# Gelu and gate product of the expert rows in groups of two instead of eight

## What is computed

```python
def peer_ffn(h, w_q, keys, u, v):
    ...                      # queries, keys, top-k: for each token 8 heads x 16 experts = 128 ids and gates g
    def block(args):
        xt, et, gt = args
        act = jax.nn.gelu(jnp.einsum('td,thkd->thk', xt, u[et]), approximate=False)
        return jnp.einsum('thk,thkd->td', gt * act, v[et])
```

## Time and profile before

| | us |
|---|---|
| median of 3 runs | 4148.64 |
| lowest, highest | 4130.71, 4150.37 |
| the profiled execution | 4132.56 |
| its span (first to last instruction) | 4130.5 |
| PE / DVE / ACT / POOL busy | 3102.1 / 2438.0 / 823.3 / 2296.8 |

### The profile page before, as it was taken

One profiled execution on the slowest core, in us unless ns is written; L12 is line 12 of the kernel. 1 busy time (PEld: TensorE's weight loads), 2 busy tenths in 40 slices (PEclk: granted clock), 3 DMA queues, 4 the chain that ended last, 5 costly groups with the idle time before them and its releaser, 6 DMA issues.

```text
span 4130.5 us, 44027 instructions
## 1 busy us (share of the span) xinstructions
PE 3102.1 (75%) x11080; PEld 1750.8 (42%) x11080; DVE 2438.0 (59%) x5947; ACT 823.3 (20%) x1936; POOL 2296.8 (56%) x2101
## 2 busy tenths in 40 slices
PE   6864788668875888677885688757897578876666
PEld 5453345253442535354452545425454344532222
DVE  5236654947467565756558474675647656476444
ACT  2100321114111221113211141112311123111111
POOL 1004675646655575556755466554566556566776
PEclk9976899889987999888998899878898799988888
DMA  6447899898998899898998889988899888989998
GB/s 219 129 128 252 311 383 374 303 339 319 386 344 312 322 385 377 310 343 320 373 362 311 323 317 376 339 317 300 301 386 341 311 298 308 398 316 334 360 365 322
DMA packets 425232, 1333.42 MB, mean 323 GB/s; under 512 B 47616, under 2 KB 48768, under 8 KB 424320
## 3 DMA queue, kind: packets, MB, share of 16 engines
q0 software_dynamic: 294912, 1073.87, 70.4%
q1 hardware_dynamic: 128896, 252.28, 17.1%
q10 hardware_dynamic: 1152, 4.19, 0.3%
HBM read 1320.46 MB, written 9.70 MB: 322 GB/s over the span
## 4 chain that ended last, share of the span: by engine, by line
PE 42%; DVE 21%; issue 19%; DMA 9%; ACT 4%; another core or an unknown queue 3%; POOL 2%; DVEq 0%; POOLq 0%; ACTq 0%; SPq 0%
PE ps_sum L990 20%; PE ps_p L771 9%; DMA rows<-in_peer_v,ids_v 4%; DVE rows L1692 4%; PE ps_s L912 4%; DMA w_ring<-in_wstream 3%; DVE feat_b L1595 3%; DVE feat_b L1590 2%; PE ps_s L855 2%; DVE e L1597 1%; PE ps_p L863 1%; POOL rows L591 1%; POOL rows L582 1%; PE ps_t L762 1%
## 5 line engine op out<-in xcount | busy, mean ns | idle before, releaser
L990 PE MATMUL ps_sum<-rows,diag 128*128 128x512 f32 x3584 | 1864.5, 657 | 561.6 <-ACT diag L1230 405.4
L582 POOL DMA_INDIRECT rows<-in_peer_u,ids_u x1024 | 1128.2, 1102 | 1231.4 <-issue 584.3
L591 POOL DMA_INDIRECT rows<-in_peer_v,ids_v x1024 | 1152.1, 1125 | 584.0 <-issue 311.0
L1692 DVE CUSTOM_DVE_ANT_0 rows<-rows,h_cur 128x1024 f32<-128x1024 f32 x1024 | 1224.0, 1221 | 182.6 <-DMA rows<-in_peer_u,ids_u 156.5
L990 PEld LDWEIGHTS ps_sum<-rows,diag 128*128 128x128 f32 x3584 | 710.6, 211 | 1445.6 <-issue 1033.8
L771 PEld LDWEIGHTS ps_p<-hT,w_ring 128*128 128x128 f32 x3968 | 513.7, 207 | 128.5 <-issue 90.0
L771 PE MATMUL ps_p<-hT,w_ring 128*128 128x128 f32 x3968 | 524.4, 292 | 47.1 <-DMA w_ring<-in_wstream 29.9
L1230 ACT ACTIVATE diag<-ident,acts 128x128 f32<-128x128 f32 x896 | 317.5, 392 | 818.0 <-PE ps_sum L990 327.2
L762 PE MATMUL ps_t<-ident,xs 128*128 128x128 f32 x192 | 45.1, 412 | 263.0 <-DVE xs L1404 183.3
L1707 DVE SCALAR_TENSOR_TENSOR x_cur<-rows,acts,x_cur 128x1024 f32<-128x1024 f32 x128 | 164.4, 1285 | 119.6 <-DMA rows<-in_peer_v,ids_v 111.1
L1500 DVE CUSTOM_DVE_ANT_0 e<-ps_s,bias_t 128x512 f32<-128x512 f32 (+3 forms) x96 | 82.2, 856 | 235.5 <-PE ps_s L851 108.7
(11 more groups left out here) (263 smaller groups left out, 2372.2 us busy)
## 6 DMA issues: line engine op xcount, KB each, us to landing
w_ring<-in_wstream SPq DMA_DIRECT2D x816, 256.0 KB
bias_t<-bias_rows SPq DMA_DIRECT2D x40, 512.0 KB
rows<-in_peer_u,ids_u POOLq DMA_INDIRECT x1024
rows<-in_peer_v,ids_v POOLq DMA_INDIRECT x1024
bias_rows<-rows SPq DMA_DIRECT2D x5, 1024.0 KB, 9.5
bias_t<-in_x SPq DMA_DIRECT2D x8, 512.0 KB
out<-x_cur ACTq DMA_DIRECT2D x8, 512.0 KB
e<-in_final_gain SPq DMA_DIRECT2D x7, 512.0 KB
```

Source lines behind the costliest of these rows:

```text
L582: pool.indirect_dma_start(u_rows[:, j % G_RING, :], None, peer_u, bass.IndirectOffsetOnAxis(ap=ids_u[:, j:j + 1], axis=0)).then_inc(u_land ...
L591: pool.indirect_dma_start(v_rows[:, j % G_RING, :], None, peer_v, bass.IndirectOffsetOnAxis(ap=ids_v[:, j:j + 1], axis=0)).then_inc(v_land ...
L990: ins = pe.matmul(ps_sum[:, c * 512:(c + 1) * 512], diag[:, n % 4, :], v_rows[:, j % G_RING, c * 512:(c + 1) * 512], start=(n == 0), stop= ...
L1692: dve.tensor_tensor_reduce(row, row, h_cur[:, :], 1.0, 0.0, ALU.mult, ALU.add, dots[:, p:p + 1]).then_inc(u_used, 1)
```

## The change

`STEP`, the size of a group of Gelu and gate product, goes from 8 to 2, and the three lags that were written as `STEP` plus a number are written as the numbers that they had. So 64 Gelus and 64 products are made in a block instead of 16 each, each of 2 columns instead of 8, and the positions of dot product, diagonal, sum and gather stay. `GATE_LAG` stays 1.

```diff
-STEP = 8
+STEP = 2
...
-DIAG_LAG = STEP + 2
-SUM_LAG = STEP + 3
-GATHER_LAG = STEP + 4
+DIAG_LAG = 10
+SUM_LAG = 11
+GATHER_LAG = 12
```

## The result

The changed kernel takes 4204.7 us in the median of four runs (4199.76 to 4215.87) beside 4149.51 us (4130.71 to 4155.33) for the kernel before, a ratio of 1.0157 with an interval of 1.0125 to 1.0189. It is slower, inside the range of 4120 to 4255 us, and by more than the forecast said: +55 us between the medians and +67.4 us between the profiled spans (4197.9 against 4130.5), where the sum gave +37. The ratio is the recorded one; the two medians alone would give 1.0133, which lies inside its interval.

What follows compares the result with a forecast made beforehand. No engine is full; a PE, DVE, ACT chain bounds attention, PE the mixing, DVE the choice. Gates 25, attention 7 and choice 5 gave 37 us on 4132.56: 4169.6 us, 4186 on the median's scale; range 4120 to 4255 us.

Steps and rivals of the forecast that it cites:

- the forecast case: Whole kernel: slower by +21 to +60 us, given a chance of 0.45.
- Gates: Gates and recurrence: a diagonal waits behind row 27's Gelu, L829 3.6 us later per block; 25 us, bounds 9 and 46.
- Attention: Six other table loads per block, 7.7 us of ACT, mostly hidden: 1 us a block, 7 us in all, bounds 0 and 54.
- The cover of the loads: Attention: loads are free where ACT waits anyway, 46.6 us in 9 of 12 Exps, so 1 us a block.
- The wait for the dot product: ACT: diagonals wait for dot products instead of gate products, four times as often; no gain booked, cost only in the gates.
- Choice: Choice of top-k: nine more products on a full DVE at 0.08 us, 5 us over seven passes, upper bound 10.
- the rival on locks: ACT stands behind copies waiting for PE, at projections and two query products, holding DVE: 74 us more; chance 0.13.
- Start of a block: DVE finishes rows 8 and 9 2.3 us later, but weights get the queues: 0 taken, bounds -21 and +35 us.
- Hidden anyway: Rival: the gates' 3.6 us is regained before the scores or at block start; 4145 or 4161 us, chance 0.30.
- Faster: Rival: products seven positions ahead free PE, a quarter of ACT's 233.7 us returns; -46 us, about 4102 us, chance 0.12.
- Every load and every lock counts: Rival: DVE is held by ACT behind copies waiting for PE, 74 us more; 4244 or 4260 us, chance 0.13.
- The other sign of being wrong: Outside the choice: the forecast is wrong if PE's idle time in front of diagonals does not grow.

Runs made afterwards that it cites:

- lock8: Kernel before plus, on ACT at each odd position, a wait for that row's dot product; no load, Gelu or product added: 4158.54 us, ratio 1.0066.
- loads8: Kernel before plus a Gelu of constant data, waiting for nothing, at each odd position without its own; 180 table loads: 4162.16 us, ratio 1.0077.
- c2: Changed kernel (groups of two) with a plain copy in place of the Gelu, 34 table loads, output not the reference's: 4167.68 us, ratio 1.0083.
- c8: Kernel before (groups of eight) with a plain copy in place of the Gelu, 34 table loads, output not the reference's: 4104.6 us, ratio 0.9935.
- mid8: Changed kernel with rows 24 to 63 back in groups of eight, groups of two elsewhere: 4156.65 us, ratio 1.0046.
- prod6: Changed kernel with each gate product four positions later, Gelus unmoved: 4238.79 us, ratio 1.0206.
- c_both2: Changed kernel with copies for Gelus, the copy three positions later and the product four behind it: 4153.95 us, ratio 1.0025.

## Why the prediction came out as it did

**Right in sign and range, short in size.** It said +37 us with +21 to +60 as the forecast case; the medians say +55, the ratio 4149.51 x 0.0157 = 65 us, and the profiled executions 67. So it lies in the forecast case by the medians alone. That it comes so near has some luck in it: the terms for attention and choice were short by 53 and 11 us in the profile, and 35 us that the sum didn't have came off at the start, in the projections, in join and mixing and behind the choice.

**Gates: right, and for the reason given.** Forecast 3.6 us in a block and 25 us in all; measured 3.43 us in the block that was followed (12.56 - 9.13) and 24 us in all, of which PE's new idle time is 3.0 us in every block and the rest its clock. The steps held one by one: the diagonal starts 0.14 us after row 27 is done (2913.44 + 1.22 = 2914.66; 0.3 was taken), PE 0.44 us behind it (0.51), L829 3.29 us behind that (3.39). lock8 shows the same split without the loads. That the wait for row 27 swallows the loads' 1.3 us is right too: alone they cost 7 us (loads8), beside the wait nothing that can be seen (PE is idle 7.98 us ahead of the first sum in the changed kernel and in lock8 alike).

**Attention: the term that failed.** It was 7 us and is 60. Two steps of it were wrong, and they account for the new idle time in latent attention; for the rest the cause stays open.
- *The cover of the loads.* "ACT waited 46.6 us in 9 of 12 Exps": a load is free there only if nothing that waits stands between the idle time and the load. In the changed order a Gelu does, as the rows at 2925.87 show, and where the load stands in front of a diagonal, PE's slack pays for it (2961.28). loads8 is 25 us longer there without any wait added, 3.6 us in a block, in the middle of the bounds of 0 and 7.7 and not near the lower end; 13.6 us of it are new idle time of PE. The size of the waits was no reason to take that end.
- *The wait for the dot product was costed once, in the gates.* For the rest I wrote that it "changes its name and comes four times as often" and booked nothing. The attention has the same chain, DVE's dot product, ACT, PE: lock8 adds 25 us there, c2 over c8 27.6 us.

In latent attention PE's idle time shows both: +13.6 us by the loads alone and +6.9 us by the wait alone are 20.5 us, and the change has +20.6 us. The stage has another 13.9 us of longer busy time.

The clock goes with it. In the two attentions PE's idle time rose by 30 us over the seven passes, and its busy time by 30 us for the same matmuls. In the stretch shown the granted clock fell from 0.87 to 0.84 as the idle time grew. That the new gaps brought the lower clock is likely in latent attention but isn't shown: loads8 has 13.6 us of new gaps there and no longer busy time. In differential attention (+26.0 us: 9.4 idle, 16.6 busy) mid8 has +25.6 us (7.2 and 18.4) with groups of eight, so what the change costs there apart from what comes out of the stages ahead of it is open. Whether loads and wait together make up the 60 us, as 25.1 and 25.1 us alone would nearly have it, can't be said either.

**Choice: a wait was missing.** Forecast 5 us, upper bound 10, measured 16.3. The products were sized right (6.1 us; prod6: 6.4; there are ten more in a choice, not nine). Not seen was that DVE waits for the first Gelu of the choice behind a copy that waits for PE; the rival on locks named the two query products and the projections as such places, not this one.

**Start of a block: 0 taken, -18.5 us in the profile,** inside the bounds of -21 and +35. The mechanism "the weights get the queues to themselves" is what the waits for weights show (29.9 to 21.0 us, at the starts 19.9 to 4.3), and prod6 is its inverse. How much it gives the whole is open.

**The rivals.** "Hidden anyway" is out. "Faster" was half right: PE's waits for diagonals did fall, from 217.6 to 208.2 us in the choices and from 43.7 to 2.3 us behind a choice up to the end of the block's experts, 51 us together. But in the choice DVE sets the pace (busy 613 of 637 us before), and the stage behind it became only 5.5 us shorter. In the gates and the two attentions they rose by 49 us, in projections, join and mixing they fell by 11. That is why the total, 405 to 390 us, told nothing. "Every load and every lock counts" had the right causes and the wrong place: it put 74 us on copies of the projections, and the stages with those became shorter. The Trainium skill, ScalarE: Activation LUTs, section "Table sets: the hidden batching unit", advises to batch activations by set; loads8 agrees, with 32 us for 56 loads and the small Gelus. By the 2.66 us a switch that the Trainium skill, ScalarE: Activation LUTs, gives in section "What ACT_TABLE_LOAD costs" the 56 loads would be an estimated 149 us of ACT. The trace shows the next instruction 1.30 us after a load's start (2378.13 to 2379.43) and the next load 0.21 us behind that, so here the drain isn't seen.

**The signs to look for.** Loads 52 to 87, 512 products of 155 ns, ACT's waits for products gone and those for dot products up by 513 us, the split of the eight matmuls, the last stretch unchanged: all as written. The choice is longer by 2.3 us in a block instead of 1. DVE's waits for Gelus rose from 55.0 to 122.7 us and POOL's for dot products from 560.8 to 698.3, twofold and by a quarter, short of the several times over that would have made the forecast wrong. The other sign of being wrong was badly chosen. PE's waits for diagonals outside the choice did not grow, as it asked: 405.4 - 217.6 = 187.8 us before, 390.4 - 208.2 = 182.2 us now. They grew, from 144.1 to 179.9 us, only if the stage behind the choice is left out too. By its letter this sign spoke against a forecast that came true, since it added up stages with different limits.

**Open.** By loads8 the added loads cost 0.77% alone; by (changed / before) / (c2 / c8) they cost 0.1%, with an uncertainty of 0.5% that I work out from the three intervals (changed, c2 and c8). Either they overlap with the added waits outside the attention, or c8 gained something of its own in the mixing. And groups of two without loads and with both waits loosened (c_both2 over c8) still cost 0.9%, of which the product's wait, what is left of the dot product's, the products in the choice (6.9 us) and the start were seen.

## What to carry to other kernels

Making a small step finer on an engine between two others buys earlier results and pays with more places where that engine stands for its source in front of work that needs nothing new: for every added instruction with a wait, list what is queued behind it and who waits for that, in each stage, and not only in the stage where it is seen first. In this case a table load was hidden only by idle time that lay directly in front of it in its engine's program. Read waits by stage, and idle time apart from busy time: here a total that stood still (405 to 390 us) was a fall of 51 us in and behind the choice, where it gave little, and a rise of 49 us in gates and attentions, where it cost. And before a stage's loss is put down to what was added in it, run the kernel with nothing added there: mid8 lost as much in differential attention without it.

## What the runs showed of the hardware

- A table load takes 1283 ns in every group, and a function that waits for nothing starts 1.29 to 1.30 us after the load's start; with 180 instead of 124 of them and 384 Gelus of two columns, which nobody waits for, the kernel took 0.77% longer, 0.57 us for each load if all of it is put on the loads. With 34 instead of 124 it took 0.65% less, 0.30 us for each.
- Expert rows that are asked for later let PE's weights come sooner, though what the kernel gains by it is not settled: holding back two expert rows at the start of a block cut PE's waits for weights from 29.9 and 28.6 us to 21.1 and 16.8 us in two profiles each, and asking for them at once (prod6) raised them to 47.6 us.
- One 128x2 product on DVE takes 155 ns and a 128x8 product 163 ns; ten more of them in each of seven choices cost 6.4 us in prod6, 0.09 us each.
- Four matmuls of the same shape (128x512) took 3.78 us at a granted clock of 0.50 (1.2 GHz) and 1.98 us at 1.00 (2.4 GHz), in one block of lock8, the first four behind 7.98 us of idle time and the second four behind 1.62 us; in the changed kernel the second four ran at 0.54 and took 3.45 us although only 1.64 us of idle time lay ahead of them.
